# Recurrent block in pairs of rows, recurrent and gate tiles in turn

## What is computed

```python
gate_br, rnn_br = split(x @ w_in_c, 2)               # 1024 -> 2 * 1024
xc, new_buf = causal_dwconv(rnn_br, conv_buf, w, b)  # width 4
r = sigmoid(blockdiag(xc, w_gate_a) + b_gate_a)      # 8 blocks of 128 x 128
i = sigmoid(blockdiag(xc, w_gate_x) + b_gate_x)
log_a = 8 * r * log_sigmoid(lru_lambda); a = exp(log_a)
b = sqrt(-expm1(2 * log_a)) * (i * xc)
h[t] = a[t] * h[t-1] + b[t]
out = (gelu(gate_br) * h) @ w_out_c
```

## Time and profile before

| | us |
|---|---|
| median of 3 runs | 1551.11 |
| lowest and highest | 1545.39, 1553.11 |
| profiled execution, its time | 1546.14 |
| profiled execution, its span | 1544.3 |
| mean granted clock of PE in it | 0.983 |
| PE, DVE, ACT, POOL busy | 1457.0, 853.8, 639.0, 61.0 |

### The profile page before, as it was taken

One profiled execution on the slowest core, in us unless ns is written; L12 is line 12 of the kernel. 1 busy time (PEld: TensorE's weight loads), 2 busy tenths in 40 slices (PEclk: granted clock), 3 DMA queues, 4 the chain that ended last, 5 costly groups with the idle time before them and its releaser, 6 DMA issues.

```text
span 1544.3 us, 24581 instructions
## 1 busy us (share of the span) xinstructions
PE 1457.0 (94%) x10352; PEld 1416.7 (92%) x10352; DVE 853.8 (55%) x1314; ACT 639.0 (41%) x1012; POOL 61.0 (4%) x80
## 2 busy tenths in 40 slices
PE   6999999999899999999999798888899999999994
PEld 6989898989799999999999697878899999999993
DVE  4556564656754544543446676867655444534456
ACT  4342524343553313331333747944733133312334
POOL 0010100000210000000000300000200000000000
PEclk9999999999999999999999899999999999999997
DMA  6131221213122222222222021112122222222212
GB/s 248 42 107 62 82 85 59 98 57 102 51 83 83 69 96 73 79 95 79 72 72 88 33 96 42 55 55 69 64 76 80 90 74 83 83 82 82 74 65 78
DMA packets 35935, 122.12 MB, mean 79 GB/s; under 512 B 4080, under 2 KB 6256, under 8 KB 35568
## 3 DMA queue, kind: packets, MB, share of 16 engines
q1 hardware_dynamic: 33264, 111.63, 20.9%
q0 software_dynamic: 2560, 8.91, 2.0%
HBM read 112.83 MB, written 7.70 MB: 78 GB/s over the span
## 4 chain that ended last, share of the span: by engine, by line
PE 81%; ACT 8%; DVE 6%; issue 4%; DMA 1%; POOL 0%; SPq 0%; POOLq 0%; DVEq 0%; ACTq 0%
PE PS L434 25%; PE PS L435 25%; PE PS L436 24%; ACT Y L800 2%; PE PS L527 2%; ACT whi L681 1%; PE PS L565 1%; DVE S L1098 1%; PE PS L545 1%; DVE Y L1195 1%; DVE Y L1192 1%; PE PS L612 1%; ACT L931 1%; PE PS L580 1%; DMA Y<-xT 1%
## 5 line engine op out<-in xcount | busy, mean ns | idle before, releaser
L434 PE MATMUL PS<-xhi,whi 128*128 128x296 f32 x2176 | 669.7, 308 | 25.6 <-DVE wlo L974 7.5
L435 PE MATMUL PS<-xlo,whi 128*128 128x296 f32 x2176 | 656.6, 302 | 0.0
L436 PE MATMUL PS<-xhi,wlo 128*128 128x296 f32 x2176 | 653.7, 300 | 0.0
L434 PEld LDWEIGHTS PS<-xhi,whi 128*128 128x128 f32 x2176 | 414.1, 190 | 40.7 <-POOL xlo L426 20.0
L435 PEld LDWEIGHTS PS<-xlo,whi 128*128 128x128 f32 x2176 | 414.4, 190 | 1.3 <-issue 0.3
L436 PEld LDWEIGHTS PS<-xhi,wlo 128*128 128x128 f32 x2176 | 413.5, 190 | 0.0
L967 DVE TENSOR_TENSOR wlo<-raw,whi 128x1024 fp32r<-128x1024 f32 (+1 forms) x198 | 238.3, 1204 | 108.1 <-ACT whi L681 104.6
L434 PE MATMUL PS<-hhi,whi 128*128 128x296 f32 x960 | 289.4, 301 | 8.6 <-ACT S L941 7.5
L435 PE MATMUL PS<-hlo,whi 128*128 128x296 f32 x960 | 288.7, 301 | 0.0
L436 PE MATMUL PS<-hhi,wlo 128*128 128x296 f32 x960 | 287.7, 300 | 0.0
L681 ACT ACTIVATE whi<-raw 128x1024 fp32r<-128x1024 f32 (+1 forms) x198 | 206.5, 1044 | 174.9 <-PE PS L436 166.0
(11 more groups left out here) (198 smaller groups left out, 1166.2 us busy)
## 6 DMA issues: line engine op xcount, KB each, us to landing
raw<-weights SPq DMA_DIRECT2D x182, 512.0 KB, 3.2
raw<-weights SPq DMA_DIRECT2D x16, 384.0 KB, 2.9
Y<-xT SPq DMA_DIRECT2D x8, 296.0 KB, 9.8
yT<-Y SPq DMA_DIRECT2D x16, 148.0 KB, 1.8
S<-s_hgrn POOLq DMA_DIRECT2D x4, 512.0 KB, 5.2
S<-s_ret POOLq DMA_DIRECT2D x4, 512.0 KB, 5.5
hgrn_out<-S POOLq DMA_DIRECT2D x4, 512.0 KB, 3.9
ret_out<-S POOLq DMA_DIRECT2D x4, 512.0 KB, 3.8
```

What stands on the lines that cost most here:

```text
L434: pe.matmul(dst, wh, h, start=first, stop=False)
L435: pe.matmul(dst, wh, lo, start=False, stop=False)
L436: return pe.matmul(dst, wl, h, start=False, stop=last)
```

## The change

The gate and recurrent tiles go in turn, two by two, with gate tiles two behind. The rows `m` are handled in four pairs `p` by one chain of instructions 1184 columns wide (`pair`), except for what differs per row: gate tanh, log_a's scale, gelu and convolution. `S` grows from 10 to 13 rows. The gate products of row `m` come after the tile that `GATES_AFTER` names. In `decay`, tanh comes before exp, and for pairs 0 and 3 gelu of gate tiles stands between them. The scan runs over both rows at once, with `a` set to zero at the start of each. `h_hi` and `h_lo` become `r_hi` and `r_lo` for this block, counted by pairs. The stream of weights is put in the new order.

```diff
+def mixer_order():
+    order = [("r", 0), ("r", 1)]
+    for m in range(2, KT, 2):
+        order += [("r", m), ("r", m + 1), ("g", m - 2), ("g", m - 1)]
+    return order + [("g", KT - 2), ("g", KT - 1)]
+MIXER = mixer_order()
+GATES_AFTER = {2: 0, 3: 1, 5: 2, 6: 3, 9: 4, 10: 5, 12: 6, 13: 7}
...
+            first_tiles(U_RNN, 1)
+            pe.wait_ge(gw_loaded, 16)
+            for i in range(2, len(MIXER)):
+                gemm(U_RNN + i, xhi, xlo)
+                if i in GATES_AFTER:
+                    gates(GATES_AFTER[i])
+            gemm(U_OUTC, hhi, hlo, r_lo, 0, both=True, per=2)
...
             def gates_of(m):
+                if m >= 2:
+                    act.wait_ge(hsc, m // 2)
...
+            def decay(p):
+                act.wait_ge(la, p + 1)
+                done(act.activation(pair(AP), pair(RP), ACT.Tanh, scale=-1.0))
+                if p in (0, 3):
+                    gelu_of(2 * p)
+                done(act.activation(pair(RP), pair(RP), ACT.Exp), aa)
+                if p == 3:
+                    gelu_of(2 * p + 1)
+                act.wait_ge(w2, p + 1)
+                done(act.activation(pair(AP), pair(AP), ACT.Sqrt, scale=0.25), mult)
...
+            for i, (kind, m) in enumerate(MIXER):
+                weights_hi(U_RNN + i + 2)
+                if kind == "r":
+                    branch(U_RNN + i, m)
+                else:
+                    if m not in (0, 6, 7):
+                        gelu(U_RNN + i, m)
+                    if i in (5, 9, 15):
+                        mix_high(m // 2)
+                if i in GATES_AFTER:
+                    gates_of(GATES_AFTER[i])
+                if i == 13:
+                    mix_high(2)
+                if GATES_AFTER.get(i, 0) % 2:
+                    decay(GATES_AFTER[i] // 2)
...
+            def recurrence(p):
+                dve.wait_ge(aa, p + 1)
+                done(tt(h, a, a, ALU.mult))
+                done(stt(r, h, 1.0, r, ALU.add, ALU.mult), w2)
+                done(tt(t8, by_row(RP)[:, :, first], h0, ALU.mult))
+                done(dve.memset(by_row(RP)[:, :, first], 0.0))
+                done(dve.memset(by_row(RP)[:, :, 0:1], 0.0))
+                dve.wait_ge(mult, p + 1)
+                done(tt(i, i, r, ALU.mult))
+                done(tt(by_row(IP)[:, :, first], by_row(IP)[:, :, first], t8, ALU.add))
+                done(dve.tensor_tensor_scan(h, a, i, 0.0, ALU.mult, ALU.add), hsc)
...
+            for i, (kind, m) in enumerate(MIXER):
+                weights_lo(U_RNN + i + 2)
+                if kind == "r":
+                    convolve(m)
+                elif m % 2:
+                    gated(m // 2, U_RNN + i)
+                    if m // 2 >= 2:
+                        mix_low(m // 2)
+                if i in (6, 10):
+                    mix_low(i // 4 - 1)
+                if GATES_AFTER.get(i, 0) % 2:
+                    log_a(GATES_AFTER[i] // 2)
+                    recurrence(GATES_AFTER[i] // 2)
```

More of the change, by code:

```diff
@@ L54 @@
 U_RNN = U_FFN0 + N_FFN
-U_GBR = U_RNN + KT
-U_OUTC = U_GBR + KT
+U_OUTC = U_RNN + 2 * KT
 U_FFN1 = U_OUTC + KT
@@ L215, in trunk @@
         Y = sb("Y", [P, KT, T])
-        S = sb("S", [P, 10, SCRW])
+        S = sb("S", [P, 13, SCRW])
         V = sb("V", [P, 2, BLK + 1, P])
@@ L285, in trunk @@
         pads = sem("pads_ready")
+        r_hi, r_lo = sem("recurrent_rows_hi"), sem("recurrent_rows_lo")
         xc_ok = sem("xc_ready")
@@ L332, in s, with pair @@
             return S[:, i, a:b]
+        def pair(i, j=None, n=1):
+            two = S[:, i:i + 2, :].rearrange("p a b -> p (a b)")[:, 0:2 * T]
+            return two if j is None else two[:, j * T:(j + n) * T]
         def at_row(n):
@@ L436, in products, with gemm @@
                 return pe.matmul(dst, wl, h, start=False, stop=last)
-            def gemm(u, hi, lo, k_ready=None, k0=0, both=False, side=None):
+            def gemm(u, hi, lo, k_ready=None, k0=0, both=False, side=None, per=1):
                 n = unit_tiles(u)
@@ L443, in gemm @@
                     if k_ready:
-                        pe.wait_ge(k_ready, k0 + k + 1)
+                        pe.wait_ge(k_ready, k0 + k // per + 1)
                     cols = slice(k * P, k * P + P)
@@ L628, in ffn @@
                     elif kind == "d":
-                        gemm(ub + i, hhi, hlo, h_lo, (FT + KT) * layer + first)
+                        gemm(ub + i, hhi, hlo, h_lo, FT * layer + first)
                     elif i == 0:
@@ L643, in _, with gates @@
             ffn(0)
[L644 to L648, removed]
+            def gates(m):
                 pe.wait_ge(xc_ok, m + 1)
@@ L892, in _, with branch @@
             ffn(0)
[L894 to L897, removed]
+            def branch(u, m):
                 wait_full(u)
@@ L913, in gates_of @@
             def gates_of(m):
+                if m >= 2:
+                    act.wait_ge(hsc, m // 2)
                 for g in range(2):
                     act.wait_ge(gate_ps, 2 * m + g + 1)
-                    done(act.activation(halves(s(gate_row(m, g))), PS[:, 4 + 2 * g:6 + 2 * g, 0:HT], ACT.Tanh,
+                    done(act.activation(halves(pair((RP, IP)[g], m % 2)), PS[:, 4 + 2 * g:6 + 2 * g, 0:HT], ACT.Tanh,
                                         scale=0.5, bias=lam[:, (5 + g) * KT + m:(5 + g) * KT + m + 1]), gate_sb)
-            def mix_high(m):
-                act.wait_ge(hmul, m + 1)
-                done(act.activation(hhi[:, m, :], s(8), ACT.Copy), h_hi)
@@ L924, in _ @@
-            act.wait_ge(half_b, 1)
[L925 to L941, removed]
@@ L942, in _ @@
-            mix_high(KT - 1)
+            def decay(p):
[8 more added lines that the diff above has]
+                done(act.activation(pair(AP), pair(AP), ACT.Sqrt, scale=0.25), mult)
@@ new lines, in gelu, with gelu_of, mix_high @@
+            def gelu(u, m):
+                wait_full(u)
+                if m >= 2:
+                    act.wait_ge(r_lo, m // 2)
+                done(act.activation(halves(pair(GEL, m % 2)), acc[u % 2][:, :, 0:HT], ACT.Gelu_apprx_tanh),
+                     free[u % 2], u // 2 + 1)
+            def gelu_of(m):
+                gelu(U_RNN + MIXER.index(("g", m)), m)
+            def mix_high(p):
+                act.wait_ge(hmul, p + 1)
+                done(act.activation(hhi[:, 2 * p:2 * p + 2, :].rearrange("p a b -> p (a b)"), pair(GEL), ACT.Copy), r_hi)
@@ new lines, in _ @@
+            act.wait_ge(pads, 2)
+            act.wait_ge(half_b, 1)
+            for i, (kind, m) in enumerate(MIXER):
[13 more added lines that the diff above has]
+                    decay(GATES_AFTER[i] // 2)
@@ L1215, in ffn @@
                 ub = U_FFN0 if layer == 0 else U_FFN1
-                hb = layer * (FT + KT)
+                hb = layer * FT
                 for r in range(2):
@@ L1315, in _, with convolve @@
                 done(dve.memset(S[:, r, 0:CW - 1], 0.0), pads if r else None)
-            for m in range(KT):
-                weights_lo(U_RNN + m + 2)
+            def convolve(m):
                 dve.wait_ge(u_sb, FT + m + 1)
-                r, t = S[:, m % 2, :], S[:, 2 + m % 2, :]
+                r, t = S[:, m % 2, :], S[:, 2, :]
                 n = LU - CW + 1
@@ L1330, in _ @@
                 done(stt(batches(Y[:, m, NP:T]), tail(r)[:, :, q:], w, tail(t)[:, :, 0:NS], ALU.mult, ALU.add), xc_ok)
[L1331 to L1367, removed]
@@ L1368, in _, with by_row, log_a @@
-            mix_low(KT - 1)
+            def by_row(i):
+                return pair(i).rearrange("p (a t) -> p a t", a=2)
+            def log_a(p):
+                dve.wait_ge(gate_sb, 4 * p + 4)
+                for j in range(2):
+                    m = 2 * p + j
+                    r = pair(RP, j)
+                    done(ts(r, r, 1.0, lam[:, KT + m:KT + m + 1], ALU.add, ALU.mult), la if j else None)
+                y = Y[:, 2 * p:2 * p + 2, :].rearrange("p a b -> p (a b)")
+                done(stt(pair(IP), pair(IP), 1.0, y, ALU.add, ALU.mult))
@@ new lines, in recurrence @@
+            def recurrence(p):
+                a, i, r, h = pair(RP), pair(IP), pair(AP), pair(SCAN)
+                first = slice(NP, T, NS)
+                t8 = lbc[:, 0:2 * NB].rearrange("p (a b) -> p a b", a=2)
+                h0 = par("h0", 2 * p * NB, 2 * NB).rearrange("p (a b) -> p a b", a=2)
+                dve.wait_ge(aa, p + 1)
[8 more added lines that the diff above has]
+                done(dve.tensor_tensor_scan(h, a, i, 0.0, ALU.mult, ALU.add), hsc)
+                done(dve.tensor_copy(out_small("h_p", 2 * p, 2), by_row(SCAN)[:, :, NP - 1]))
+                done(dve.tensor_copy(out_small("h_s", 2 * p * NB, 2 * NB).rearrange("p (a b) -> p a b", a=2),
+                                     by_row(SCAN)[:, :, NP + NS - 1:T:NS]))
@@ new lines, in gated, with mix_low @@
+            def gated(p, u):
+                free_of(u - 1)
+                free_of(u)
```

(14 more changed lines are left out.)

## The result

The changed kernel takes 1565.71 us (median of 4 runs, 1563.66 to 1567.0), the kernel before 1548.25 (4 runs, 1544.26 to 1553.11). The ratio is 1.0106, 95% interval 1.0084 to 1.0127: slower by 1.1%.

The account below looks back on a forecast made before the run. PE bounds the kernel, busy 94%; only its waits can give time. 1005.7 without waits + 31.0 gaps + 7.7 clock = 1044.4 for the pair's end, against 1029.3: 15.5 added to 1548.9 came to 1564.5 us, range 1550 to 1576.

Parts of the forecast that it names:

- The gaps: PE waits for low halves behind the recurrence before tiles 6, 9, 13 and the output pair, together 31.0 us.
- tile 17's 0.3: Before the output pair: 0.3 us for tile 17's low half, on top of 10.4 us.
- the chain of tile 9: From tile 6's end to tile 9's low half: 22.6 us against PE's 15.1, a gap of 7.5.
- The fourth gap: Before the output pair: decay(3) through tile 16's low half, 10.4 us, and 0.3 for tile 17's.
- the order on DVE: Low halves of 6, 9, 13 and 16 stand behind the recurrence on in-order DVE, so PE waits for the pair's chain.
- Prices of wide rows: Pair instructions 1184 wide: 1.20 us on ACT, 1.39 on DVE, 2.63 for the scan, before handover.
- Table loads: In the stage, ACT's loads fall from 24 to 14 if tanh needs none behind gelu; 12.9 us of ACT's time.
- The clock: PE's clock falls to half about 4 us into each of four gaps, 1.9 us lost each, 7.7 in all.
- The first one, PE's pace: Faster: chains fit beneath the tiles, the three inner gaps vanish, 11 us less, 1538; chance 7%.
- The second, low prices: About the same: all prices at their low ends, clock falling in fewer gaps, +4, 1553; chance 5%.
- The dear switch: A table switch costs 1.37 us more than its row; 12 fewer, 16 us, so 1548; chance 2%.
- A wait that was not seen: ACT or the transfers could add an unseen wait, making it slower still, inside the range; no separate chance given.

Follow-up runs that it names:

- the first experiment: Changed kernel with high and low halves of tiles 6, 9, 13 and 16 moved ahead of the pair's chain: 1547.89 us, 0.9986 of the kernel before.
- the third experiment: Changed kernel with each pair's scan done twice on DVE, same result: 1573.14 us.
- the second experiment: Changed kernel with gelu of gate tile 0 taken out of decay(0) into iteration 4 of its own: 1561.79 us.
- the last but one experiment: Changed kernel with low halves, gelu of gate tile 0, gates and evacuation of tiles 5 and 7 moved out of the chain: 1529.66 us, 0.9884 of kernel before.
- the fourth experiment: Changed kernel with the decay's sqrt replaced by a scaled copy needing no table, four table loads fewer: 1555.39 us.

## Why the prediction was right

- **Direction and size.** 1564.5 forecast, 1565.71 measured; the stage by +15.5, measured +16.7. That the totals agree to 1.2 us is in part luck: the medians lie 17.5 apart, the start was taken 0.7 too high, and single executions of the kernel before scatter by 9 us.
- **The gaps.** 7.3, 7.5, 5.5 and 10.7 (with tile 17's 0.3) forecast; 7.59, 7.74, 5.76 and 10.68 measured. Each of the first three is 0.2 to 0.3 us short. In the chain of tile 9, a third of this is the low half: it takes 1.24 us to its end, where the forecast had 1.15, the time from its start to that of the next row on DVE. The rest is spread in hundredths over the other steps. The fourth gap agrees by luck: it was short by the same 0.3, and the 0.3 added for tile 17 did not come, as PE, at half clock, took up tile 17 at 1037.05, 0.6 us after that low half was there. That the order on DVE is the cause was argued from the code; the first and the third experiment show it, by taking the rows out and by lengthening the chain.
- **Prices of wide rows.** 1.20 on ACT, 1.39 on DVE and 2.63 for the scan were worked out from single rows; the chain shows 1.20, 1.40 and 2.63.
- **Table loads.** 14 in the stage, as counted (1 at the first gates, 5 for gelu, 4 each for exp and sqrt): tanh behind gelu needed none (gelu's load at 926.27, tanh at 934.02, next load at 947.35).
- **The clock.** 7.7 forecast for the four gaps, 7.2 measured. The rule behind it, that the fall comes 4 us into a gap, was too simple: the second experiment had it after a gap of 3.35 us.
- **What the sum did not have.** The slow spell at the start of the stage, 1.6 us, which two of the seven profiles of the new order show and neither of the two of the old one. It is the whole difference between the end of the pair that was forecast, 159.5 us after the start of the stage, and the 161.1 measured. Nothing in the stage that the change touches runs before it; what sets it off is open.
- **The rivals.** The first one, PE's pace, was wrong for this order and right for the same instructions in another: the last but one experiment has DVE at 98 us and PE at its pace. Its point of decision, a chain shorter than the tiles that cover it, need not be reached if the weights don't stand behind the chain. The second, low prices, is out as the wide rows took what was forecast. The dear switch is refuted by the fourth experiment. A wait that was not seen, of ACT or of the transfers, did not add to the sum: the four gaps account for PE's waits, and in the first experiment the three inner ones went with the place of the low halves.

## What to carry to other kernels

Before a long chain goes on an in-order engine, ask which short row behind it another engine is waiting for; a wide instruction that saves time in sum can cost its whole length on the path. Busy shares (an estimate of 25 of 30 us for DVE here) say what an order could reach, not what it does. When the unit of work doubles, the lead of its feeders (here the weights, two tiles ahead) has to grow with it.

## What was not expected of the hardware

The granted clock can fall to half after PE has taken up work again: after an idle stretch of 3.35 us at full clock, PE worked for 1.0 us at 1.00 and then for 3.5 us at 0.51. It also fell at full work at the start of the stage (3.5 us at 0.55), behind a stretch of 3.8 us in which PE had been busy for 2.1 at a clock of 1.00. All nine profiles have that stretch, alike to 0.01 us of PE's time, and seven of them have no fall behind it, so what PE did just before does not decide it alone. The doubled scan showed that a chain's length passes on to PE to 0.01 us.
